# A tile's high and low part side by side: one 512-column product in the down and last four up projections of a two-block transformer kernel

## The reference

```python
def swiglu(x, w_gate, w_up, w_down):
    return (jax.nn.silu(x @ w_gate) * (x @ w_up)) @ w_down

def swiglu_2(h, w_in, w_out):
    gate, up = jnp.split(h @ w_in, 2, axis=-1)
    return (jax.nn.silu(gate) * up) @ w_out
```

## Time and profile before

| | |
|---|---|
| median of 3 runs | 1706.29 us (1706.27 to 1710.0) |
| the profiled execution | 1708.15 us |
| its span, first to last instruction | 1706.3 us |
| mean granted TensorE clock | 0.996 of full |
| TensorE busy (matmul) | 1658.8 us, 97% |
| TensorE busy (weight load) | 1623.4 us, 95% |
| VectorE busy | 1154.4 us, 68% |
| ScalarE busy | 785.0 us, 46% |

### The profile page before, as it was taken

How to read it: one execution, slowest core, us unless ns; L and a number is a source line. 1 busy time by engine, 2 the same in 40 slices (tenths; PEclk the granted TensorE clock), 3 DMA queues, 4 the chain that set the end, 5 groups by cost and what they waited for, 6 DMA issues and landing times.

```text
span 1706.3 us, 33888 instructions
## 1 busy us (share of the span) xinstructions
PE 1658.8 (97%) x13708; PEld 1623.4 (95%) x13708; DVE 1154.4 (68%) x1472; ACT 785.0 (46%) x926; POOL 171.7 (10%) x196
## 2 busy tenths in 40 slices
PE   7899999999999999999999899999999999999998
PEld 6899998999999999999989899999999989899998
DVE  5777779777866667665687666656665577676653
ACT  1444445354544455444463554445444554454431
POOL 3000113600000000000052100000000034200000
PEclk9999999999999999999999999999999999999999
DMA  8988897655776576656642466568665743366653
GB/s 309 266 268 253 260 305 237 212 167 156 198 193 175 153 198 192 190 153 167 205 125 99 129 174 192 156 173 215 193 172 162 213 149 100 99 164 183 180 155 107
DMA packets 496976, 315.58 MB, mean 185 GB/s; under 512 B 14015, under 2 KB 487850, under 8 KB 495978
## 3 DMA queue, kind: packets, MB, share of 16 engines
q1 hardware_dynamic: 487604, 282.34, 57.7%
q0 software_dynamic: 8288, 30.15, 5.1%
q10 hardware_dynamic: 982, 1.64, 0.3%
HBM read 313.04 MB, written 1.05 MB: 184 GB/s over the span
## 4 chain that ended last, share of the span: by engine, by line
PE 81%; DVE 10%; ACT 3%; DMA 2%; SPq 2%; issue 2%; POOL 0%; DVEq 0%; ACTq 0%; POOLq 0%
PE accs L1626 22%; PE accs L1628 22%; PE accs L1627 22%; DVE wlo L978 3%; PE wide L1663 1%; PE wide L1661 1%; PE accs L1663 1%; PE accs L1661 1%; PE wide L1662 1%; PE accs L1662 1%; DVE wlo L987 1%; PE wide L1832 1%; DMA in_turn<-in_w_ada 1%; PE bank L1725 1%; SPq L482 1%
## 5 line engine op out<-in xcount | busy, mean ns | idle before, releaser
L1626 PE MATMUL accs<-uhi_shift,whi 128*128 128x256 f32 x2304 | 652.7, 283 | 7.0 <-DVE ulo L1027 5.7
L1628 PE MATMUL accs<-uhi_shift,wlo 128*128 128x256 f32 x2304 | 648.6, 282 | 0.0
L1627 PE MATMUL accs<-ulo,whi 128*128 128x256 f32 x2304 | 645.1, 280 | 0.0
L696 ACT CAST whi<-raw 128x2048 fp32r<-128x2048 f32 (+2 forms) x294 | 499.4, 1701 | 106.8 <-PE accs L1628 61.2
L978 DVE TENSOR_TENSOR wlo<-raw,whi 128x2048 fp32r<-128x2048 f32 (+2 forms) x251 | 500.7, 2003 | 10.4 <-ACT whi L696 6.2
L1626 PEld LDWEIGHTS accs<-uhi_shift,whi 128*128 128x128 f32 x2304 | 435.2, 189 | 13.0 <-issue 10.2
L1627 PEld LDWEIGHTS accs<-ulo,whi 128*128 128x128 f32 x2304 | 437.1, 190 | 1.2 <-issue 1.2
L1628 PEld LDWEIGHTS accs<-uhi_shift,wlo 128*128 128x128 f32 x2304 | 435.1, 189 | 0.0
L1626 PE MATMUL accs<-hhi,whi 128*128 128x256 f32 x1120 | 318.5, 284 | 1.9 <-DVE wlo L978 1.5
L1628 PE MATMUL accs<-hhi,wlo 128*128 128x256 f32 x1120 | 317.6, 284 | 0.0
L1627 PE MATMUL accs<-hlo,whi 128*128 128x256 f32 x1088 | 308.6, 284 | 0.0
(11 more groups left out here) (321 smaller groups left out, 2213.4 us busy)
## 6 DMA issues: line engine op xcount, KB each, us to landing
raw<-in_ffn_w_in SPq DMA_DIRECT2D x176, 512.0 KB, 5.1
in_turn<-in_w_ada POOLq DMA_DIRECT2D x56, 512.0 KB, 5.7
raw<-in_w_mix_in SPq DMA_DIRECT2D x52, 512.0 KB, 4.7
raw<-in_ffn_w_out SPq DMA_DIRECT2D x64, 384.0 KB, 3.6
raw<-in_w_ff_gate SPq DMA_DIRECT2D x44, 512.0 KB, 4.2
raw<-in_w_ff_up SPq DMA_DIRECT2D x44, 512.0 KB, 5.6
raw<-in_w_in SPq DMA_DIRECT2D x40, 512.0 KB, 5.0
raw<-in_ffn_w_out SPq DMA_DIRECT2D x64, 320.0 KB, 4.0
```

The source lines that it names most:

```text
L696: nc.scalar.copy(whi[:, n % RING, 0:cols], raw[:, n % RING, 0:cols]).then_inc(hi_ready, 1)
L1626: mm(dst, wh, xh, start=first, stop=False)
L1627: mm(dst, wh, xl, start=False, stop=False)
L1628: return mm(dst, wl, xh, start=False, stop=last)
```

## The change

In all six downs and in the ups of FFN 2 to 5, the high and low part of a tile lie side by side in one buffer (`u_parts`, `hid_parts`; two rows of 258 columns, of which 256 are read). The helper `paired` replaces `three`: one matmul of 512 columns multiplies the high weight with both parts, into 512 PSUM columns; a second of 256 columns adds the low weight times the high part into the first half. The two halves of the bank are added when the result is taken out:

- in the ups, each half (gate, up) now has a bank of its own. ScalarE copies the second halves of both banks to `gate_up` (128x512), VectorE adds the first halves to it, then multiplies by `rstd` in a further instruction; the step for the low part of tile t moves into VectorE's step t+1 (`low_of`).
- in the downs, VectorE's add into `h` is done twice, once for each half, and the second waits for the first.

FFN 0 and 1's ups, the mixers and the output projections keep `three`.

```diff
-        uhi_shift = sb("uhi_shift", [P, KD, T + 2], F32R)
+        u_parts = sb("u_parts", [P, KD, 2, T + 2], F32R)
+        uhi_shift, ulo = u_parts[:, :, 0], u_parts[:, :, 1, 0:T]
...
+        hid_parts = hidden.enter_context(nc.sbuf_tensor("hid_parts", [P, KF, 2, T + 2], F32R))
+        hhi, hlo = hid_parts[:, :, 0, 0:T], hid_parts[:, :, 1, 0:T]
...
@@ ScalarE, up step, i >= 2
-                        act.wait_ge(evacuated, it * RING + 2 + e0 + t + 1)
-                        nc.scalar.activation(pair[:, 0], pair[:, 0], ACT.Silu, ...).then_inc(silu_ready, 1)
-                        split_ahead(n0 + t, it)
+                            act.wait_ge(hlo_ready, it * RING + KF * i + t - 1)
+                            act.wait_ge(chunk_used, it * RING + RING + n0 + t + 1)
+                            nc.scalar.copy(pair, bank_pair(t)[:, :, T:2 * T]).then_inc(half_taken, 1)
+                            split_ahead(n0 + t, it)
+                            act.wait_ge(pair_scaled, it * RING + KF * (i - 2) + t + 1)
+                            nc.scalar.activation(pair[:, 0], pair[:, 0], ACT.Silu).then_inc(silu_ready, 1)
                         act.wait_ge(hid_ready, it * RING + KF * (i - 1) + t + 1)
                         nc.scalar.copy(dst, pair[:, 1]).then_inc(hhi_ready, 1)
@@ VectorE, up step, i >= 2
-                        nc.vector.tensor_tensor(pair, ps, by_token(2), ALU.mult).then_inc(evacuated, 1)
+                            dve.wait_ge(half_taken, it * RING + KF * (i - 2) + t + 1)
+                            nc.vector.tensor_tensor(pair, banks[:, :, 0:T], pair, ALU.add).then_inc(evacuated, 1)
+                            dve.wait_ge(evacuated, it * RING + 2 + e0 + t + 1)
+                            nc.vector.tensor_tensor(pair, pair, by_token(2), ALU.mult).then_inc(pair_scaled, 1)
+                            if t or not isinstance(it, int):
+                                low_of(t - 1, it)
                         if t or not isinstance(it, int):
                             split_ahead(n0 + t, it)
@@ VectorE, down, after an odd chunk
+                        nc.vector.scalar_tensor_tensor(out=hm, in0=acc[(e0 + m) % 2][:, T:2 * T], scalar=gm, in1=hm,
+                                                       op0=ALU.mult, op1=ALU.add).then_inc(half_added, 1)
+                        dve.wait_ge(half_added, it * 2 + KD * i + m + 1)
                         nc.vector.scalar_tensor_tensor(out=hm, in0=acc[(e0 + m) % 2][:, 0:T], scalar=gm, in1=hm,
                                                        op0=ALU.mult, op1=ALU.add).then_inc(evacuated, 1)
@@ TensorE
+            def paired(dst, wh, wl, parts, first, last):
+                mm(dst.rearrange("p (a t) -> p a t", a=2), wh, parts[:, :, 0:T], start=first, stop=False)
+                return mm(dst[:, 0:T], wl, parts[:, 0, 0:T], start=False, stop=last)
...
+            def paired_tiles(n, banks, e=None, waits=None):
+                vh, vl = kview(whi, n % RING, KD, 256), kview(wlo, n % RING, KD, 256)
+                order = (0, 1) if e is None or e % 2 == 0 else (1, 0)
+                for ks in (range(KD), ) if waits is None else (range(KD - 2), range(KD - 2, KD)):
+                    for j in order:
+                        c = slice(j * P, (j + 1) * P)
+                        if e is not None and j == order[1]:
+                            bank_free(e + 1)
+                        for k in ks:
+                            if waits is not None and j == order[0]:
+                                pe.wait_ge(ulo_ready, waits + k + 1)
+                            ins = paired(banks[:, j], vh[:, k, c], vl[:, k, c], u_parts[:, k], k == 0, k == KD - 1)
+                return ins
...
@@ TensorE, down
-                            pe.wait_ge(hlo_ready, KF * i + KF // 2 * (side + 1))
+                            pe.wait_ge(hlo_ready, KF * i + (KF - 1 if side else KF // 2))
...
-                            ins = three(acc[(e0 + m) % 2][:, 0:T], vh[:, k], vl[:, k], hhi[:, kk], hlo[:, kk],
-                                        kk == 0, kk == KF - 1)
+                            if t == 1 and kk == KF - 1:
+                                pe.wait_ge(hlo_ready, KF * i + KF)
+                            ins = paired(acc[(e0 + m) % 2], vh[:, k], vl[:, k], hid_parts[:, kk], kk == 0, kk == KF - 1)
```

More of the change, by code:

```diff
@@ L245, in build @@
         hidden = ExitStack()
-        hhi = hidden.enter_context(nc.sbuf_tensor("hhi", [P, KF, T], F32R))
-        hlo = hidden.enter_context(nc.sbuf_tensor("hlo", [P, KF, T], F32R))
+        hid_parts = hidden.enter_context(nc.sbuf_tensor("hid_parts", [P, KF, 2, T + 2], F32R))
         hidden.close()
+        hhi, hlo = hid_parts[:, :, 0, 0:T], hid_parts[:, :, 1, 0:T]
+        merged = ExitStack()
+        merged_a = merged.enter_context(nc.sbuf_tensor("merged_a", [P, KF, T], F32R))
+        merged_b = merged.enter_context(nc.sbuf_tensor("merged_b", [P, KF, T], F32R))
+        merged.close()
         lv = sb("lv", [P, TT, 512])
@@ L281, in bank_pair @@
             return (accs, wide)[t % 2][:].rearrange("p (a c) -> p a c", a=2)
-        merged_hi = [hhi[:, (0, 2, 12, 14)[kk]:(0, 2, 12, 14)[kk] + 2] for kk in range(4)]
-        merged_lo = [(hhi, hlo)[kk // 2][:, 16 + 2 * (kk % 2):18 + 2 * (kk % 2)] for kk in range(4)]
+        merged_hi = [merged_a[:, (0, 2, 12, 14)[kk]:(0, 2, 12, 14)[kk] + 2] for kk in range(4)]
+        merged_lo = [(merged_a, merged_b)[kk // 2][:, 16 + 2 * (kk % 2):18 + 2 * (kk % 2)] for kk in range(4)]
         ident = const[:, C_IDENT:C_IDENT + P]
@@ L1140, in ffn, with low_of @@
                 n0, e0 = seg(f"up{i}")
+                def low_of(t, it=0):
+                    dve.wait_ge(hhi_ready, it * RING + KF * i + t + 1)
+                    src = hid[:, t % 2] if i == 0 else gate_up[:, t % 2, 1]
+                    nc.vector.tensor_tensor(tiles_of(hlo, t, it, RING), src, tiles_of(hhi, t, it, RING).bitcast(F32),
+                                            ALU.subtract).then_inc(hlo_ready, 1)
                 def step(t, it=0):
@@ L1172, in step @@
                         ins.then_inc(hid_ready, 1)
-                    dve.wait_ge(hhi_ready, g)
-                    src = hid[:, t % 2] if i == 0 else gate_up[:, t % 2, 1]
-                    nc.vector.tensor_tensor(tiles_of(hlo, t, it, RING), src, tiles_of(hhi, t, it, RING).bitcast(F32),
-                                            ALU.subtract).then_inc(hlo_ready, 1)
+                    if i < 2 or isinstance(it, int) and t == KF - 1:
+                        low_of(t, it)
                 if i:
@@ L1767, in step @@
                     bank_free(e0 + t, it, RING)
+                    first = t == 0 and isinstance(it, int)
                     if i == 1:
-                        first = t == 0 and isinstance(it, int)
                         ins = shift_tiles(n0 + t, bank_pair(t), e0 if first else None, waits if first else None)
-                    elif t == 0 and isinstance(it, int):
+                    elif i:
+                        ins = paired_tiles(n0 + t, bank_pair(t), e0 if first else None, waits if first else None)
+                    elif first:
                         ins = first_tiles(n0, acc[e0 % 2], waits)
```

18 lines of the change are left out of this document (11 added, 7 removed).

## The result

The changed kernel takes 1721.42 us (median of 4 runs, 1718.91 to 1724.38), the kernel before in the same comparison 1708.01 us (1706.27 to 1710.0). The ratio is 1.0078 with a 95% interval of [1.0064, 1.0091]: slower by 13.4 us. The forecast was 1697 us with a range to 1716, so size and sign were wrong. The rival "the long product saves nothing" gave 1723 us at 7%. The profiled execution took 1721.85 us with a span of 1720.2.

The account below looks back on a forecast made before the run. TensorE bounds the kernel before (busy 1658.8 of 1706.3 us). FFN 0 +1.5; FFN 1 +0.9 less 0.5; FFN 2 -1.0 + 2.3; FFN 3, 4 each -3.5 + 0.9; FFN 5 -3.5 - 3.6: about -9, 1697 us, range 1683 to 1716.

Parts of the forecast that it names:

- the long product saves nothing: Rival, 7%: 512-column product equals two 256-column halves; down tiles 8.38 us, ups as before, 1723 us in all.
- the 10 ns above 107 ns: TensorE step: 256-column excess is load against stream, which 512 columns avoid; triple 0.334 us instead of 0.353 or 0.360.
- The 0.216: TensorE's assumed time in us for one 512-column product, from the pace of long moving operands in the earlier trace.
- upper bound of 0.343: TensorE's triple in us if 10 to 13 ns stay with every product; as a rival 15%, 1706 us.
- down 5: Last down, without `uhi`: chain 3.0 us hidden under 3.70, tile 7.40 us, so -3.6 us over seven tiles.
- The second add in the downs: Tile boundaries: 0.62 us more before the low weights, ready at 4.27; tile 8.12 us instead of 7.92.
- Down 2: Down with one more instruction in its boundary chain, already waiting: tile 8.75 us instead of 8.4, +2.3 us.
- the round: Ups 2 to 5: closed VectorE and ScalarE loop, 5.62 us a step, above TensorE's 5.35, setting 12 of 22 steps.
- the first rival: Rival, 12%: TensorE stays the bound in the ups, round 5.35 us or less; 1684 us in all.
- Up 2: TensorE already waits 0.61 us for the first multiply; sum of squares 0.5 us later, so gain only 1.2 us.
- The rest of the edit I cost at nothing: Side-by-side buffers and the first up tile's wait for the last down add: no cost; without cover 0.2 us a segment.

Follow-up runs that it names:

- narrow probe: Kernel before with side-by-side buffers and other product sizes in downs 1, 3, 4, 5; only steps read: 0.117, 0.06, 0.0325, 0.11 us.
- Low weights first: The changed kernel with VectorE's low weights for the next odd chunk made before its wait for the tile's end: 1698.02 us, ratio 0.9934.
- the first experiment: The kernel before with high and low parts side by side in rows of 258 columns, still three products and no added instructions: 1713.43 us, ratio 1.0027.
- the ups alone: The changed kernel with its downs back to three products and one add, last-hidden-tile wait at the second chunk's start: 1715.0 us, ratio 1.0046.
- the wait mended: The changed kernel with downs back to three products and one add, last-hidden-tile wait ahead of the last triple: 1711.29 us, ratio 1.0012.

## Why the prediction was wrong

**The step that failed: "the 10 ns above 107 ns look like load and stream getting in each other's way, and a 512-column product should not pay them".** The load of 0.11 us is hidden: with a quarter of the weights the 256-column product still steps at 0.117. The 10 ns are something else. By the narrow probe some 6 of them lie in the columns (256 at 0.44 ns are 113, not 107 ns), and a product twice as long pays them twice; some 4 belong to each product. The 512-column product costs 0.232 to 0.234 us, not 0.216, and the triple 0.3515 us, not 0.334. The 0.216 came from float32 products in the earlier trace rows. The `xqk` row steps at 0.43 us for 512 columns, 0.84 ns a column, which I counted as two passes of 0.42; no run shows how many passes a row holds, and I carried that pace to another type. The triples themselves had the right one in plain sight (0.353 / 768 = 0.46 ns a column). My upper bound of 0.343 was too low for the same reason: it assumed that the excess is paid once for each product, and more than half of it is paid for each column. With 0.3515 for 0.334 and all else as written, an up gives 336 x 0.0018 = 0.6 us, down 5 gives 1.2, and a tile of downs 1, 3 and 4 is the 8.2 to 8.4 of the rival.

The Trainium skill's TensorE: Matmul & The Clock Gate (Back-to-back issue gap) would have the 512-column product at 216 ns, or at 131 in a stream; in this stream it is 0.232 to 0.234 us, so neither holds here.

**The second add in the downs: right, and it became the price.** I had the low weights ready at 4.27 us after the even chunk's start and a tile of 8.12 us; the trace has 1339.72 - 1335.53 = 4.19 and 8.21. The add is 0.52 us, not 0.62, and the even chunk longer than forecast (3.85 us, not 3.70). Low weights first turn +13.4 us into -10 against the kernel before. Not all of the -10 is the change's: the same line moved in the kernel before gives 7, and the paired downs on top of that another 6. That the boundary in down 2 was a cost before the change was in the earlier trace rows; I used it as a check of the sum and did not see it as something to remove.

**Down 2** I had at +2.3 and it took +3.4 (66.2 to 69.6 inside); **down 5** -3.6 and -1.2 us, the product's size again.

**The ups: the round is no bound.** I had 5.62 us for the round, from hops of 0.13 to 0.16 in the loop. VectorE in a loop step of up 4, then ScalarE from the copy for this step to the copy for the next:

```profile
1216.09 0.69 DVE L1181 TENSOR_TENSOR work<-accs,work 128x512 f32<-128x512 f32 x1 [1.34 <-ACT work L783]
1216.81 0.69 DVE L1183 TENSOR_TENSOR work<-work,rstd 128x512 f32<-128x512 f32 x1
1217.42 0.42 DVE L1159 TENSOR_TENSOR hid_parts<-work,hid_parts 128x256 f32 x1
1217.76 2.28 DVE L992 TENSOR_TENSOR wlo<-raw,whi 128x2048 fp32r<-128x2048 f32 x1
1219.96 0.42 DVE L1195 TENSOR_TENSOR work<-work 128x256 f32<-128x256 f32 x1
```

```profile
1215.47 0.59 ACT L783 COPY work<-accs 128x512 f32<-128x512 f32 x1 [0.18 <-PE accs L1658]
...
1220.51 0.41 ACT L789 CAST hid_parts<-work 128x256 f32 x1 [2.33 <-DVE work L1195]
1221.10 0.59 ACT L783 COPY work<-wide 128x512 f32<-128x512 f32 x1 [0.18 <-PE wide L1658]
```

The copy starts 0.26 us after `hhi`'s cast could have ended (1220.51 + 0.33), and it is TensorE that releases it. The pieces sum to 0.72 + 0.61 + 0.34 + 2.20 + 0.55 + 0.33 + 0.59 + 0.03 = 5.37 us; the hop from ScalarE to VectorE is 0.03 us (1215.47 + 0.59 to 1216.09). TensorE needs 16 x 0.3515 = 5.62 us and sets the pace. That equals my number for the round, by accident. The copy's 0.59 us is what I took (0.60). This was the first rival's mechanism, and with the product as it is it brings nothing.

**Up 2** I had at -1.2 and it took +2.1 inside. TensorE's waits with their starts:

```profile
662.00 0.47 PE L1657 MATMUL accs<-u_parts,whi 128*128 128x512 f32 x1 [1.19 <-DVE work L1181]
668.68 0.51 PE L1657 MATMUL wide<-u_parts,whi 128*128 128x512 f32 x1 [0.83 <-DVE wlo L992]
...
681.22 0.49 PE L1657 MATMUL wide<-u_parts,whi 128*128 128x512 f32 x1 [1.01 <-DVE wlo L992]
```

The first add came late with the sum of squares, as forecast: TensorE waits 1.2 us, where it waited 0.6. Not forecast were the 1.8 us of two waits for low weights in the steps right behind it, which start late too. The second of them follows a reciprocal of 1.75 us for the final norm, which stands in VectorE's list in this up alone (`L1106`, at 673.88). My sum had one round for every up and did not go through up 2's own list. In the other ups the same late start costs no wait.

**"The rest of the edit I cost at nothing"** failed: the side-by-side rows of `u` cost 1.1 us in each of ups 3 to 5 and those of the hidden tiles give back 0.4 to 0.7 a down. With what came in FFN 0 the rows made 5 us (the first experiment). Of that, part is the clock. Up 1 starts at 458.04 us in the kernel before, with 3.4 us at half clock ahead of it, and at 462.30 with the rows alone, with 10.2. In "the ups alone" it starts at 458.77 (3.4 us at half clock), in the same kernel with the wait mended at 462.03 (10.2 us). By the 0.4 us for each us of the mixers above, 6.8 us more would make some 2.7 of such a difference, an estimate.

**The balance.** Laid side by side by the starts of their segments, the two profiled executions differ by 13.9 us: +3.6 before up 1 starts, +0.3 in up 1, +9.4 from down 1 to 4 (2.1, 3.4, 1.9 and 2.0), +2.1 in up 2, -1.65 in ups 3 to 5, +0.9 in the two later mixers, -0.65 in down 5 and the end. The change had 20.4 us at half clock and the kernel before 13.6 (the last stretch, behind the work, left out), so some 2.7 of the 13.9 are an estimate of the clock's part, and no run shows that the change brought it about. By the medians of different runs, good to some 2 us: rows side by side +5 (a part of it the clock's), second add and paired product in the downs +11, paired ups -3; in sum +13, as measured. Without the clock's part the loss stays: most of it is the waits in the downs.

**What stays open.** Why an `fp32r` product streams a column in 0.44 ns where the float32 ones show 0.84; why the place of the moving rows is worth 1% of a stretch, in either direction; and what decides how long the clock stays at half in the mixers and in FFN 0. No run took these apart.

## What to carry to other kernels

Before two products are merged into one longer one, divide the step by its columns in the same type and see whether load or columns set it. Here all loads were hidden, and merging saved 5 to 8 ns of 355 a triple. When a change adds an instruction behind a tile's end, ask which work in that queue does not need the tile and move it ahead: this gained 7 us without the change and 23 with it. Before a difference of a few us is given to a change, compare the time at half clock in the parts that it leaves alone. An experiment that holds one part of a change must hold the waits that belong to it as well.

## What the runs showed of the hardware

With a narrow load, an `fp32r` product costs 0.44 ns for each moving column and some 4 ns besides, from 64 to 512 columns (0.0325, 0.06, 0.117 and 0.23 us). With a full load, 256 columns step at 0.117 to 0.120 us and 512 at 0.232 to 0.234, with VectorE and ScalarE idle or at work, and 128 columns at 0.11, as long as the load alone. The float32 products of the earlier trace rows show 0.84 ns a column. The same instructions ran 1% slower in the ups and 1% faster in the downs when only the place of the buffers changed.

TensorE's granted clock went between 1.00 (2.4 GHz) and 0.50 (1.2 GHz). In down 4 of the narrow probe it fell after TensorE, busy all of the 21.5 us before the down, had been busy 2.80 of 6.3 us. In one and the same mixer, 10.2 us at half clock in place of 3.4 made 147.09 us of 144.44.
